# RG-LRU stage: two of four gate products on GpSimd, splits and scan inputs in another order

## The reference

```python
gate_branch, rec = jnp.split(x @ w_in, 2, axis=-1)
gate_branch = gelu(gate_branch)
u = causal_depthwise_conv4(rec)
r = sigmoid(blockdiag(u, w_a) + b_a);  i = sigmoid(blockdiag(u, w_x) + b_x)
log_a = -8 * r * softplus(-lam);  a = exp(log_a)
b_in = sqrt(-expm1(2 * log_a)) * (i * u)
h[t] = a[t] * h[t-1] + b_in[t]            # over the 256 tokens
return (h * gate_branch) @ w_o            # the gate products, then w_o: 1280 x 1024
h = layer_norm(ALPHA * h_in + mix)        # then the MLP
```

## Time and profile before

| | |
|---|---|
| median of 3 runs | 2067.94 us (2067.27 to 2068.09) |
| profiled execution, span from first to last instruction | 2067.1 us (0.8 below the runs' median; no other time of it is recorded) |
| TensorE matmul, busy | 2047.0 us, 99% |
| VectorE | 1540.0 us, 75% |
| ScalarE | 1054.1 us, 51% |
| GpSimd | 170.6 us, 8% |
| mean granted TensorE clock | 0.998 |

### The profile page before, as it was taken

The page is one execution under the profiler, slowest core; times in us unless marked ns, Lnnn a source line. Parts: engine busy times, 40 slices in busy tenths (PEclk is TensorE's granted clock), DMA queues, the critical chain, the costliest instruction groups (busy, mean ns, idle before and its releaser), DMA issues.

```text
span 2067.1 us, 26974 instructions
## 1 busy us (share of the span) xinstructions
PE 2047.0 (99%) x11155; PEld 1755.9 (85%) x11155; DVE 1540.0 (75%) x1704; ACT 1054.1 (51%) x1236; POOL 170.6 (8%) x94
## 2 busy tenths in 40 slices
PE   8999999999999999999999999999999999999998
PEld 6988888898988888778888988888888888788887
DVE  6888899789978767666766787666876667567665
ACT  5574655456565545455433665344654345455432
POOL 2001121020112105000000000000000005000000
PEclk9999999999999999999999999999999999999999
DMA  8544555564455556555665555655366556455653
GB/s 279 173 139 167 185 193 190 181 195 143 143 194 194 184 184 193 169 183 183 206 197 180 177 186 184 220 183 149 142 202 206 192 183 210 143 186 181 212 196 102
DMA packets 244739, 377.67 MB, mean 183 GB/s; under 512 B 14101, under 2 KB 179210, under 8 KB 244618
## 3 DMA queue, kind: packets, MB, share of 16 engines
q1 hardware_dynamic: 244474, 375.42, 55.2%
q10 hardware_dynamic: 144, 0.52, 0.1%
HBM read 374.87 MB, written 1.05 MB: 182 GB/s over the span
## 4 chain that ended last, share of the span: by engine, by line
PE 92%; DVE 4%; DVEq 1%; ACT 1%; DMA 0%; issue 0%; SPq 0%
PE bank L738 46%; PE acc L738 44%; PE bank L736 2%; DVE slot_lo L2043 2%; DVEq L2038 1%; ACT slot_hi L1510 1%; PE acc L736 0%; DMA slot<-in_w_in 0%; DVE arena L2798 0%; DVE arena L2300 0%; DVEq L2302 0%; DVE arena L2804 0%; DVE arena L2132 0%; ACT arena L1505 0%; DVE arena L2419 0%
## 5 line engine op out<-in xcount | busy, mean ns | idle before, releaser
L2043 DVE TENSOR_TENSOR slot_lo<-slot,slot_hi 128x2048 fp32r<-128x2048 f32 (+1 forms) x343 | 787.9, 2304 | 271.0 <-ACT slot_hi L1510 270.1
L1510 ACT ACTIVATE slot_hi<-slot 128x2048 fp32r<-128x2048 f32 (+1 forms) x343 | 650.4, 1904 | 379.2 <-DMA slot<-in_mlp_w 310.1
L738 PE MATMUL acc<-slot_hi,split 128*128 128x512 f32 x2236 | 713.2, 392 | 4.8 <-DVE slot_lo L2043 3.1
L738 PE MATMUL bank<-split,slot_hi 128*128 128x512 f32 (+1 forms) x2292 | 536.2, 366 | 0.3 <-ACT arena L1505 0.3
L738 PEld LDWEIGHTS acc<-slot_hi,split 128*128 128x128 f32 x2236 | 420.9, 188 | 93.8 <-issue 5.7
L738 PEld LDWEIGHTS bank<-split,slot_hi 128*128 128x128 f32 x2292 | 403.7, 189 | 62.0 <-issue 1.5
L738 PE MATMUL acc<-slot_lo,split 128*128 128x512 f32 x1118 | 436.7, 391 | 0.0
L738 PE MATMUL bank<-split,slot_lo 128*128 128x256 f32 x2022 | 320.7, 282 | 0.0
L738 PEld LDWEIGHTS bank<-split,slot_lo 128*128 128x128 f32 x2022 | 290.8, 191 | 17.1
L738 PEld LDWEIGHTS acc<-slot_lo,split 128*128 128x128 f32 x1118 | 210.7, 188 | 41.0 <-issue 1.0
L738 PE MATMUL bank<-slot_hi,split 128*128 128x512 f32 (+1 forms) x804 | 218.4, 380 | 1.2 <-ACT split L1527 0.9
(11 more groups left out here) (249 smaller groups left out, 1541.0 us busy)
## 6 DMA issues: line engine op xcount, KB each, us to landing
slot<-in_mlp_w SPq DMA_DIRECT2D x128, 1024.0 KB, 5.4
slot<-in_ret_w_in SPq DMA_DIRECT2D x48, 1024.0 KB, 5.2
slot<-in_w_up SPq DMA_DIRECT2D x40, 1024.0 KB, 5.1
slot<-in_w_in SPq DMA_DIRECT2D x37, 1024.0 KB, 5.3
slot<-in_w_down SPq DMA_DIRECT2D x22, 1024.0 KB, 4.9
slot<-in_ret_w_o SPq DMA_DIRECT2D x16, 1024.0 KB, 4.9
slot<-in_lru_w_in SPq DMA_DIRECT2D x10, 1024.0 KB, 5.4
slot<-in_w_out SPq DMA_DIRECT2D x8, 1024.0 KB, 4.9
```

Source lines behind the costliest of these rows:

```text
L738: i = nc.tensor.matmul(o, w, m, start=start, stop=stop)
L1510: A(whi[u.r][:, 0:u.cols], raw[u.r][:, 0:u.cols], ACT.Copy).then_inc(slot_hi[u.r], 1)
L2043: TTO(wlo[u.r][:, 0:u.cols], raw[u.r][:, 0:u.cols], f32(whi[u.r][:, 0:u.cols]), ALU.subtract)\
```

## The change

Four edits. Gate products 1 and 3 (tiles 2 to 5, and 8 and 9) move from VectorE to GpSimd, with two new semaphores: `lru_scanned` (VectorE, raised by scans 4 and 5, then by scans 8 and 9) and `lru_pooled` (GpSimd, raised by each product). `high_rows` waits for `lru_pooled` for the odd groups. ScalarE splits `lwo` 4 ahead of `high_rows(3)` and not behind it. On VectorE the split of `lwo` 1 follows the scans directly, and `inputs(1)` and the split of `lwo` 2 stand ahead of `low_rows(1)`, where they stood behind it.

```diff
@@ ScalarE @@
             def high_rows(g):
-                act.wait_ge(V["lru_product"], g + 1)
+                act.wait_ge(V["lru_pooled" if g % 2 else "lru_product"], g // 2 + 1)
                 A(lru_part(0, g), lr[:, LRU_ROWS[g], :], ACT.Copy).then_inc(V["hi_out"], 1)
@@
             high_rows(1)
             weights.ahead(slots["lwo", 0])
             high_rows(2)
+            weights.ahead(slots["lwo", 1])
             high_rows(3)
             project("lwo", 5)
@@ VectorE @@
                 for f in fs:
-                    nc.vector.tensor_tensor_scan(...)
+                    last = nc.vector.tensor_tensor_scan(...)
+                return last
@@
             low_rows(0)
-            scans((4, 5))
-            evacuated(dve, banks["lw", 7])
-            gated(1)
+            scans((4, 5)).then_inc(V["lru_scanned"], 1)
             weights.ahead(slots["lw", 8])
-            low_rows(1)
             inputs(1)
             weights.ahead(slots["lw", 9])
+            low_rows(1)
             scans((6, 7))
             evacuated(dve, banks["lw", 8])
             gated(2)
-            scans((8, 9))
+            scans((8, 9)).then_inc(V["lru_scanned"], 1)
             low_rows(2)
             weights.ahead(slots["lwo", 0])
-            evacuated(dve, banks["lw", 9])
-            gated(3)
             low_rows(3)
             project("lwo", 5)
@@ GpSimd @@
             retention(0)
+            for i, (g, c) in enumerate(((1, 7), (3, 9))):
+                fs = LRU_ROWS[g]
+                evacuated(pool, banks["lw", c])
+                pool.wait_ge(V["lru_scanned"], i + 1)
+                TTO(lr[:, fs, :], lr[:, fs, :], lgt[:, fs, :], ALU.mult).then_inc(V["lru_pooled"], 1)
             retention(1)
```

More of the change, by code:

```diff
@@ L481, in build @@
                  "conv_scaled conv_done silu_done hid_ready hid_used relu_done rot_out gn_var gn_std ro_gated "
-                 "ry_ready lru_nl lru_gelu lru_exp lru_ratio lru_root lru_product lru_y mcT_ready ckv_squared ckv_var ckv_std cn_ready "
+                 "ry_ready lru_nl lru_scanned lru_pooled lru_gelu lru_exp lru_ratio lru_root lru_product lru_y mcT_ready ckv_squared ckv_var ckv_std cn_ready "
                  "mla_max mla_probs tab_full tab_free hi_out product_ready ln_mean ln_std ln_scaled trig_ready out_ready stored").split()
@@ L2797, in scans @@
                 for f in fs:
-                    nc.vector.tensor_tensor_scan(lr[:, f, :], la[:, f, :], li[:, f, :], 0.0, ALU.mult, ALU.add)
+                    last = nc.vector.tensor_tensor_scan(lr[:, f, :], la[:, f, :], li[:, f, :], 0.0, ALU.mult, ALU.add)
+                return last
             def gated(g):
```

## The result

The changed kernel takes 2071.57 us (median of 21 runs, 2070.73 to 2072.42). The kernel before takes 2068.96 in its 21 runs (2066.97 to 2069.44). The first three of these 21 are the three runs that stood ahead of the prediction; their median lies one microsecond lower. The ratio is 1.0014, 95% interval 1.0008 to 1.0021: 2.9 us slower (1.7 to 4.3; the two medians themselves are 2.6 apart). 2.9 us is inside the 0.2% that the prediction takes as no change, and the interval leaves out any gain.

What follows compares the result with a forecast made beforehand. The prediction took TensorE to bound the kernel (92% of the chain). New stall +5.70, old stalls -3.51, clock +1.69 - 1.69 gave +2.19 us on 2067.94: 2070.1 us, range 2067.4 to 2072.2.

Steps and rivals of the forecast that it cites:

- The new stall: TensorE ahead of `lwo` 1, waiting for `low_rows(1)` behind product 1 and the split of `lwo` 2: +5.70 us.
- The old stalls: TensorE's two waits at `lwo` 3 and `lwo` 4 in the last projection would go: -3.51 us.
- The clock: TensorE's loss at the lower clock level after the stall, taken as 1.69 us, the same as before.
- The clock rival: All 24 matmuls of `lwo` 1 at the lower clock lose 5.44 us: +5.9 us, 2073.9; chance 0.10.
- Layer norm: VectorE's layer norm after the projection begins at 1232.2 instead of 1228.54; nothing counted, but no slack left.
- The sum: New stall, old stalls and clock together: +2.19 us, a shift that stays to the end.
- The base: Time before the change: the runs' median 2067.94 us, 0.8 above the profiled span, taken unchanged.
- Faster: The sign that the whole kernel gains more than the 0.2% (4.1 us) a measurement can tell; chance 0.04.
- first rival: The stalls at the projection's end go and nothing replaces them: -5.20 us, 2062.7; chance 0.04.

Runs made afterwards that it cites:

- e1: The changed kernel with `low_rows(1)` back ahead of `inputs(1)` and the split of `lwo` 2; ratio 1.0000 against the kernel before.
- e2: The changed kernel with gate product 1 back on VectorE, the changed order kept; ratio 0.9997 against the kernel before.
- e6: The changed kernel with VectorE waiting for gate product 1 ahead of the split of `lwo` 1; +1.9 us (0.0 to 3.7) against the kernel before.
- e7: The changed kernel with ScalarE's split of `lwo` 2 ahead of `high_rows(1)`; median 2069.50 us, +1.4 us against the kernel before.
- e5: e4 with VectorE's splits of `lwo` 3 and 4 moved ahead of `low_rows(2)` and `low_rows(3)`, all products on VectorE; 2065.35 us, ratio 0.9985 against the kernel before.
- e3: The changed kernel with product 1 back on VectorE and `low_rows(1)` back ahead; 2065.79 us, ratio 0.9986 against the kernel before.
- e4: The kernel before with one edit, ScalarE's split of `lwo` 4 ahead of `high_rows(3)`; 2066.56 us, ratio 0.9989 against the kernel before.
- e0: The changed kernel as it is, run again on another chip; 2071.89 us, ratio 1.0016 against the kernel before.

## Why the prediction was right

The time came out 1.5 us above the predicted 2070.1 and inside the range, with the sign and the mechanism that were forecast.

- **The new stall.** Forecast: `lwo` 1 late by 5.70 us; measured 5.60. The product was forecast at some 4.4 us (a wait behind the split and 2.28 of work), the links behind it at 0.96, 1.90, 2.20 and 1.22, and the profile has 4.44, 0.96, 1.92, 2.21 and 1.22. e1, e2, e6 and e7 each change one link and get back 4.0, 2.8, 1.4 and 1.8 us of the lateness. That the split beside it, and nothing of its own, makes the product 4.4 us long is shown by e6.
- **The old stalls.** Forecast gone, 3.51 us; they are gone. The slots asked for at 1225.3 and 1228.05 in the forecast were ready, no wait is in the profile.
- **The clock.** Taken as 1.69, the same as before; measured 1.88 and 2.36 in the two profiles of the changed kernel. The size is near by luck in part. The prediction carried over some 3.4 us at the lower level, all behind the stall; the profile has 6.8 us, of which 3.0 lie inside the stall and cost nothing. Nor did the prediction see that the low clock comes after such a stall in some executions and not in others, as e2 shows for a stall of 2.6 us. The clock rival (5.44 us lost) did not come.
- **Layer norm.** Forecast to begin at 1232.2; it began at 1233.02, which is 1232.45 with the stage's later start taken off, and TensorE did not wait for it. Its last halves ended at 1237.80 and the transposes began at 1237.55, so the slack was used up as forecast, without cost in this profile.
- **The sum.** +2.19 forecast for the stretch, +2.23 and +2.70 measured. The runs say +2.9 (1.7 to 4.3).
- **The base.** This is the weakest step: "2067.94, 0.8 above, which I take unchanged". Every other profiled execution here took 1.8 us more than its span (1.76 to 1.84), and the two later ones of the kernel before, with the same span of 2067.1 and the low clock, took 2068.89 and 2068.91. So the span belongs to an execution of about 2068.9 us, and the base was the median of three runs that lay lower, at 2067.27 to 2068.09. From 2068.9 the same sum gives 2071.1. This is 1.0 of the 1.5 us between forecast and measurement.
- **Chances.** Faster had 0.04, and nothing supports it. The first rival's -5.20 held as the most that could be won: e5 gets 3.70 of it in the stretch.

What stays open: the 21 runs of the kernel before spread over 2.5 us, seven at 2068.09 or below and fourteen at 2068.52 or above; those of e1 and e2 spread over 2.0 and 2.6, those of e3, e4 and e5 over about 1. A low clock that comes in some executions only, as shown for e2, would make such a spread. It would also explain why the runs put the change at +2.9 and the sum at +2.19, as the sum has the clock loss on both sides. The mean granted clock points the same way: of the 33 runs of the kernel before beside e0 to e3, all twelve up to 2068.33 us have 0.999, and 14 of the 21 above have 0.998. But all three profiles of the kernel before have the low clock, so for that kernel it is argued and not shown.

## What to carry to other kernels

Before moving a step ahead of another on one engine, write down what the step waits for on the other engines: here a weight split was put ahead of the last step that the next matmuls needed, and the split waited behind the very product that had just been made slower. Work taken off a full VectorE and given to GpSimd is not free where the two stand still for each other, as they did here: it came back as 2.2 us on one VectorE instruction and 1.1 on another. And a stall that a queue's order makes is best mended in that order: one line on ScalarE, inside a wait that was there anyway, gave 2.3 us.

## What was unexpected of the hardware

The same stall of TensorE (2.62 and 2.63 us, same kernel) was followed by the 1.2 GHz level in one execution and not in another, at a price of 1.62 us. Where it came, the loss did not grow with the stall: 1.73 us after 2.58, 2.89 after 3.66, 1.73 after 4.00, 1.88 and 2.36 after 5.4. The rows show why the longest stalls did not lose most: in the changed kernel the clock fell inside the stall, and about 3.0 of its 6.8 us at the lower level passed while TensorE had nothing to do. After stalls of 1.26 to 2.15 us, in the profiles of four kernels, the low clock was not seen; for one of them, e1, the spread of its runs speaks for it in some executions.
